# Order of the input stage's head, and the factor of the last norm, in a one-core decoder kernel

## Chip, core and metric

The kernel runs on one NeuronCore of one Trainium2 chip. The metric is the device time of one execution in microseconds (us), the median of several runs. Engines: PE (TensorE), DVE (VectorE), ACT (ScalarE), POOL (GpSimd), and SP, which here only issues transfers (DMAs).

## What is computed

One layer of a decoder runs over two groups of tokens that share the weights: a prompt of 1024 tokens and 8 single new tokens ("sample"). All is float32, the model width is 1024.

```python
def rmsnorm(x, g):
    return x * rsqrt(mean(x * x, -1) + 1e-6) * g

u = rmsnorm(h, norm_g) @ w_in                      # one wide projection, split into parts
o_r = rwkv_branch(first 1664 columns of u, ...)    # token-shift recurrence
o_n = nsa(...)                                     # sparse attention: compressed, selected, window
m = sigmoid(g_r) * ((o_r * silu(z_r)) @ proj_r) + sigmoid(g_n) * ((o_n * silu(z_n)) @ proj_n)
h = h + m @ w_out
h = h + sigmoid(h @ w_pg) * rmsnorm(p @ w_pe, pe_norm_g)
y = rmsnorm(h, final_norm_g)
```

The change touches the first line (the norm in front of the projection) and the last (the final norm of the prompt's last two tiles of 128 tokens).

## The kernel before

The kernel is a chain of stages (input projection, recurrence, token projection, attention, sample attention, merge, finish). Each stage is a block with a program per engine. The engines are ordered by semaphores only; a program waits with `wait_ge` and goes on in its own order. Between two stages stands one barrier, and semaphores of the stage before are cleared there (`Stage.clear`, L82). Each stage starts when the slowest engine of the one before is done.

**Input stage, `project_input`.** The tokens are nine tiles: eight of 128 prompt tokens, and one of 8. SP loads the tiles of `x`, five of the ten small vectors, and the first weights `w_z` (L751), in a queue written out by hand; ACT issues the other five vectors (L724). For each tile i:

- ACT squares the tile and sums (L938), and takes the root (L940, semaphore `rooted`).
- DVE takes the reciprocal (L1049) and scales the tile (L1051, `normed`).
- PE transposes it, eight blocks of 128x128 (`turn(i)`, L817, `turned`): four into one PSUM bank, four into the next.
- ACT copies the first four blocks to `xnT`, multiplying each by the norm's gain (L928, `out_a`); DVE copies the other four (L987, `out_v`).

The gain is a column of `vec`. The ten vectors land in `rows`, PE transposes them once (L893, `vec_t`), and DVE copies the result to `vec` (L981, `vec_o`). For the first three tiles the scaling of all three comes before the copies of all three; later tiles go one by one, and ACT and DVE copy tile i-1 behind their work on tile i.

PE then runs products of 344 tokens by 128 columns of weights over 8 blocks of the width (`product(u)`, L833); each block is two matmul instructions in the trace. The first product needs tiles 0 to 2. Turns of later tiles stand between and inside the products. Ahead of all that PE transposes the identity over and over (`keep_clock`, L122), 28 times before the vectors and 10 times behind them. Behind the plain products come pairs of products at L879.

**Finish stage, `finish_tokens`.** It goes over the tiles in four pairs. For the last pair (tiles 6 and 7; v = `NT - 2` and `NT - 1`), DVE makes the last sums of both: tile 6 in `gated_last` (L3910, L3912, `y0_l`), tile 7 in `gated` (L3901, L3903, `y0_v`), each in halves of 512 columns, the half of columns 512 to 1023 first. ACT squares each half and sums (L3776) and takes the root (L3786, `y_root`). DVE then runs `normed(v)`: the reciprocal (L3917) and two instructions of 512 columns that multiply by it and by the gain `gfin` (L3920, `y_out`). SP waits for `y_out` and stores tile by tile (L3554), the last tile in two halves (L3557). POOL has part of the sums of pairs 0 to 2 (L3851, L3853) and nothing in the last pair. `et` is a buffer of the gated rows, dead once the sums are made.

Of the kernel before, what the change touches and what calls it, by code (L numbers as in the profile page):

```python
# [15 lines left out]
ALU = mybir.AluOpType  # L16
# [3 lines left out]
P = 128  # L20
D = 1024
KC = D // P
# [24 lines left out]
NV = 51  # L47
# [621 lines left out]
def project_input(nc, k, x, o):  # L669
# [9 lines left out]
    with Stage(nc) as ctx:  # L679
# [61 lines left out]
        def turn_bank(i):  # L741
            return 6 if i == 0 or i > 2 else 6 - 2 * i
# [65 lines left out]
        def _(pe):  # L808
# [12 lines left out]
            def product(u):  # L821
# [5 lines left out]
                pe.wait_ge(out_v, last_tile + 1)  # L827
                if u >= 6:
                    pe.wait_ge(copied, u - 5)
                for c in range(KC):  # L830
                    if c == KC // 2 and u % 3 == 2 and u + 3 <= NT:
                        turn(u + 3)
                    last = nc.tensor.matmul(k.ps[:, u % 6, 0:CG], w[:, n % w_ring, c, :], k.xnT[:, c, g * CG:(g + 1) * CG],  # L833
                                            start=(c == 0), stop=(c == KC - 1))
# [56 lines left out]
            keep_clock(nc, k, 7, 28)  # L891
            pe.wait_ge(in_vec, 160)
            nc.tensor.transpose(k.ps[:, 0, 0:NV], rows[:], k.ident[0:NV, 0:NV]).then_inc(vec_t, 1)  # L893
            keep_clock(nc, k, 7, 10)
            for i in range(3):
                turn(i)
# [79 lines left out]
        def _(dve):  # L976
# [3 lines left out]
            dve.wait_ge(vec_t, 1)  # L980
            nc.vector.tensor_copy(k.vec[:], k.ps[:, 0, 0:NV]).then_inc(vec_o, 1)  # L981

            def turned_out(i):
                m = tokens(i)
                dve.wait_ge(turned, 2 * i + 2)
                for c in range(4):
                    last = nc.vector.tensor_scalar(k.xnT[:, 4 + c, i * P:i * P + m], k.ps[:, turn_bank(i) + 1, c * P:c * P + m],  # L987
                                                   k.vec[:, V_NG + 4 + c:V_NG + 5 + c], None, ALU.mult)
                last.then_inc(out_v, 1)
# [55 lines left out]
            dve.wait_ge(vec_o, 1)  # L1045
            for i in range(NT + 1):
                m = tokens(i)
                dve.wait_ge(rooted, i + 2)
# [2408 lines left out]
def finish_tokens(nc, k, x, o):  # L3457
# [8 lines left out]
    with Stage(nc) as ctx:  # L3466
# [30 lines left out]
        gm_l, y0_l = ctx.sem("gated_last"), ctx.sem("y_summed_last")  # L3497
        block = ctx.block()
# [29 lines left out]
        def _(sp):  # L3528
# [23 lines left out]
            for v in range(NT - 1):  # L3552
                sp.wait_ge(y_out, 2 * v + 2)
                sp.dma_start(o.y_prompt[0, tile_rows(v), :], h[:, v, :]).then_inc(k.y_stored[v % 2], 16)  # L3554
            for n in (1, 0):
                sp.wait_ge(y_out, 2 * NT - n)
# [278 lines left out]
        def _(pool):  # L3835
# [10 lines left out]
            for p in range(NPR - 1):  # L3846
                for n, half in enumerate((1, 0)):
# [5 lines left out]
                    nc.gpsimd.tensor_tensor(h[:, 2 * p, cols(half)], a, h[:, 2 * p, cols(half)], ALU.add).then_inc(y0_p, 1)  # L3853

        @block.vector
        def _(dve):
# [146 lines left out]
            normed(NT - 2)  # L4003
            normed(NT - 1)
# [150 lines left out]
```

## Time and profile before

| | us |
|---|---|
| median of 3 runs | 1676.46 |
| lowest and highest run | 1670.69, 1685.29 |
| the profiled execution | 1676.41 |
| its span, first to last instruction | 1674.6 |
| PE busy in the span | 1627.0 |

The mean granted TensorE clock of the span is 0.996. The busy time of an engine is the sum over its instructions; a wait is shown in front of the instruction that waited, with what released it. In a row such as `14.64 4.87 PE L833 ... x16` the first number is when the group starts, counted from the span's start, and the second how long it takes from first start to last end. "SPq" is the issue of a transfer, not its flight.

### The profile page before, as it was taken

The numbers are of one execution on the slowest core, as the hardware profiler recorded it, in microseconds if no ns is written. First come the engines' busy times: TensorE is split into PE (matmuls) and PEld (weight loads), VectorE is DVE, ScalarE is ACT, GpSimd is POOL, SyncE is SP. The second block draws the span as 40 slices with busy tenths as digits, with TensorE's granted clock in tenths as the row PEclk, the third lists the DMA queues.
The fourth block names the chain that finished last, engine by engine and source line by source line (L and its number), as shares of the span: only waits on it lengthen the run. The fifth ranks groups of instructions, "written<-read, shape, count | busy, mean of one in ns | idle before, by whom it ended". The sixth has DMA issues, their size and how long they took to land. (4 is left out here: it accounts for less than half of the span.)

```text
span 1674.6 us, 45562 instructions
## 1 busy us (share of the span) xinstructions
PE 1627.0 (97%) x20051; PEld 1163.7 (69%) x20051; DVE 854.1 (51%) x1790; ACT 577.1 (34%) x1244; POOL 396.1 (24%) x455
## 2 busy tenths in 40 slices
PE   8999999999999999999999999999999999999997
PEld 6788777777777555676767889765588888445443
DVE  3433555556565354767766664541152466624344
ACT  5221444454533114667663111223312211102444
POOL 0212223333331130556454220223100032000110
PEclk9999999999999999999999999999999999999999
DMA  5112000100101315712001975458611420700001
GB/s 169 39 50 57 3 17 16 29 17 17 29 17 36 93 29 138 218 51 101 2 2 71 293 293 197 155 139 198 157 25 27 140 62 1 277 1 1 25 26 50
DMA packets 111449, 136.80 MB, mean 82 GB/s; under 512 B 42940, under 2 KB 93829, under 8 KB 106046
## 3 DMA queue, kind: packets, MB, share of 16 engines
q1 hardware_dynamic: 102002, 84.61, 17.4%
q0 software_dynamic: 9216, 49.29, 9.5%
q8 instruction: 159, 2.61, 0.7%
q14 instruction: 36, 0.29, 0.1%
q10 hardware_dynamic: 36, 0.01, 0.0%
HBM read 121.28 MB, written 17.15 MB: 83 GB/s over the span
## 5 line engine op out<-in xcount | busy, mean ns | idle before, releaser
L1276 PE MATMUL ps<-xnT,rw_side_w 64*64 64x344 f32 x2304 | 219.3, 458 | 1.6 <-issue 0.9
L1276 PEld LDWEIGHTS ps<-xnT,rw_side_w 64*64 64x64 f32 x2304 | 97.2, 134 | 33.5 <-issue 12.4
L2744 PE MATMUL ps<-xnT,zT 128*128 128x344 f32 x384 | 120.1, 457 | 0.0
L2458 POOL TENSOR_SCALAR probs<-probs,row_sums,gates 128x63 f32<-128x63 f32 (+6 forms) x148 | 95.5, 666 | 94.9 <-DVE row_sums L2414 94.5
L2744 PEld LDWEIGHTS ps<-xnT,zT 128*128 128x128 f32 x384 | 69.5, 190 | 33.1 <-issue 3.4
L2363 ACT ACTIVATE probs<-probs,neg_max 128x63 f32<-128x63 f32 (+6 forms) x148 | 87.5, 595 | 0.3 <-DVE neg_max L2404 0.3
L2336 PE MATMUL ps<-probsT,kvtok 128*64 128x128 f32 x1056 | 76.2, 282 | 0.0
L2379 ACT ACTIVATE probsT<-ps 128x512 f32<-128x512 f32 (+1 forms) x80 | 45.9, 574 | 84.0 <-PE ps L2322 84.0
L2309 PE MATMUL ps<-kT,zT 64*128 64x512 f32 (+3 forms) x384 | 72.0, 484 | 2.2 <-DVE neg_max L2404 1.6
L3454 POOL TENSOR_TENSOR mT<-mT,gate_n 128x258 f32<-128x258 f32 x28 | 23.7, 854 | 210.9 <-DVE gate_n L3417 210.9
L2336 PEld LDWEIGHTS ps<-probsT,kvtok 128*64 128x64 f32 x1056 | 56.7, 138 | 24.2 <-issue 23.1
L2322 PE MATMUL ps<-ident,probs 128*128 128x128 f32 (+1 forms) x460 | 68.8, 281 | 4.8 <-DVE probsT L2435 3.2
L2435 DVE COPY probsT<-ps 128x512 f32<-128x512 f32 (+1 forms) x80 | 50.5, 631 | 37.3 <-PE ps L2322 36.4
L1804 POOL TENSOR_TENSOR rw_Lb<-rw_Lm,level_mask 128x512 f32<-128x512 f32 x40 | 54.0, 1359 | 49.9 <-PE ps L1458 33.0
L3353 ACT ACTIVATE zT<-ps 128x258 f32<-128x258 f32 x72 | 27.8, 387 | 106.5 <-PE ps L3335 83.7
L2322 PEld LDWEIGHTS ps<-ident,probs 128*128 128x128 f32 (+1 forms) x460 | 50.2, 141 | 17.7 <-issue 10.4
L3567 PE MATMUL ps<-w_sums,ring_k 128*128 128x512 f32 x128 | 57.2, 593 | 1.6 <-DVE h_tok L3880 1.6
L3335 PE MATMUL ps<-xnT,zT 128*128 128x258 f32 x256 | 57.6, 381 | 0.0
L1014 DVE TENSOR_TENSOR zT<-ps,zT 128x258 f32<-128x258 f32 x30 | 12.8, 426 | 82.3 <-PE ps L879 82.3
L879 PE MATMUL ps<-x_tok,z_sums 128*128 128x258 f32 x240 | 53.8, 381 | 0.0
L3335 PEld LDWEIGHTS ps<-xnT,zT 128*128 128x128 f32 x256 | 48.6, 190 | 7.1
L3880 DVE TENSOR_TENSOR h_tok<-ps,h_tok 128x512 f32<-128x512 f32 x28 | 19.3, 691 | 61.1 <-PE ps L3567 61.1
(625 smaller groups left out, 3584.6 us busy)
## 6 DMA issues: line engine op xcount, KB each, us to landing
w_z<-in_w_in_dram SPq DMA_DIRECT2D x13, 512.0 KB, 5.1
xnT_kept<-xnT SPq DMA_DIRECT2D x1, 4128.0 KB
x_tok<-in_x_prompt_dram SPq DMA_DIRECT2D x8, 512.0 KB, 7.0
rw_side_w<-in_w_in_dram SPq DMA_DIRECT2D x16, 256.0 KB, 3.4
zT<-in_w_in_dram SPq DMA_DIRECT2D x8, 512.0 KB, 6.1
ring_k<-in_w_in_dram SPq DMA_DIRECT2D x8, 512.0 KB, 5.2
w_out<-in_w_out_dram SPq DMA_DIRECT2D x1, 4096.0 KB
h_tok<-in_x_prompt_dram SPq DMA_DIRECT2D x8, 512.0 KB, 5.2
```

The source lines that it names most:

```text
L879: last = nc.tensor.matmul(k.ps[:, bank, 0:cq], left[:, c, :], right[:, c, :], start=(c == 0 and name in ("P1", "P5", "P2")), stop=(c == 3) ...
L1276: last = nc.tensor.matmul(k.ps[half(f), bank, 0:CG], w.side[half(e), g // 3 % 2, c, half(f)], k.xnT[half(e), c, third(g)], start=(phase == ...
L1804: nc.gpsimd.tensor_tensor(w.Lb[:, n % 2], w.Lm[:].rearrange("p q c n -> p (q c) n"), bc(k.tab["level_mask"][:, n + 1, :], 1, 8), ALU.mult) ...
L2309: last = nc.tensor.matmul(k.ps[:, 2 * (s % 2) + g, at:at + w], k.qT[half(g), j, i * P:(i + 1) * P], keys[half(g), t0:t0 + w], start=True, ...
L2322: last = nc.tensor.transpose(k.ps[0:m, 4 + pc % 2, (2 * b + g) * P:(2 * b + g + 1) * P], region(n, br, g, t * P, m), k.ident[:])
L2336: last = nc.tensor.matmul(k.ps[half(g), 6 + n % 2, 0:P], vals, pt[0:m, pc % NPT, (2 * b + g) * P:(2 * b + g + 1) * P], start=(br == 1 and ...
L2363: nc.scalar.activation(every, every, ACT.Exp, scale=-1.0, bias=neg_m[:, at:at + 1], accum_out=ls[:, at:at + 1]).then_inc(expd, 1)
L2435: nc.vector.tensor_copy(to, src).then_inc(pt_v, 1)
L2458: nc.gpsimd.tensor_scalar(every, every, ls[:, at:at + 1], k.gates[:, i, gate:gate + 1], ALU.mult, ALU.mult).then_inc(scaled, 1)
L2744: ins = self.nc.tensor.matmul(self.k.ps[:, self.banks[n % nb], 0:CG], self.w[:, t % 2, c, :], self.k.xnT[:, c, g * CG:(g + 1) * CG], start ...
L3335: last = nc.tensor.matmul(k.ps[:, bank, 0:CQ], stationary(u, n, name, c), moving(u, n, name, c, i), start=(c == 0 and name in ("P1", "P5", ...
L3567: last = nc.tensor.matmul(k.ps[:, bank, :], left[:, c, :], right[:, c, :], start=(first and c == 0), stop=(c == 3), skip_group_check=True)
```

## The change

In the input stage:

- PE makes 22 transposes of the identity instead of 28, then turns tile 0, then waits for the vectors and turns them, then tiles 1 and 2, then makes 8 more transposes of the identity (into bank 1) instead of the 10 that stood behind the vectors.
- DVE no longer copies the vectors before it norms the first tile, but between tiles 1 and 2.
- DVE's four copies of a tile by 128 columns become one multiply of 128x512 from PSUM, with the gain spread over the tokens.
- A product waits for ACT's half of the tiles at its start as before, but for DVE's half only in front of its fifth block.

In the finish stage, for tiles 6 and 7 only:

- They are multiplied by the gain before their roots are there: three halves on POOL (both of tile 6, the later columns of tile 7), one on DVE, all into `et`.
- DVE takes both reciprocals. POOL then scales all of tile 6 in one instruction (`y_pool`), DVE tile 7 in two halves.
- SP's store of tile 6 waits for POOL. The stores' order is the same: tile 6, then the two halves of tile 7.

The diff holds nothing about the barrier between stages; the kernel before has it already.

```diff
--- before
+++ after
@@ -824,10 +824,11 @@
                     pe.wait_ge(in_w[n % w_ring], 16)
                 last_tile = min(NT, ((g + 1) * CG - 1) // P)
                 pe.wait_ge(out_a, last_tile + 1)
-                pe.wait_ge(out_v, last_tile + 1)
                 if u >= 6:
                     pe.wait_ge(copied, u - 5)
                 for c in range(KC):
+                    if c == KC // 2:
+                        pe.wait_ge(out_v, last_tile + 1)
                     if c == KC // 2 and u % 3 == 2 and u + 3 <= NT:
                         turn(u + 3)
                     last = nc.tensor.matmul(k.ps[:, u % 6, 0:CG], w[:, n % w_ring, c, :], k.xnT[:, c, g * CG:(g + 1) * CG],
@@ -888,12 +889,13 @@
                 last.then_inc(last_t, 1)
 
             pe.wait_ge(eye_made, 1)
-            keep_clock(nc, k, 7, 28)
+            keep_clock(nc, k, 7, 22)
+            turn(0)
             pe.wait_ge(in_vec, 160)
             nc.tensor.transpose(k.ps[:, 0, 0:NV], rows[:], k.ident[0:NV, 0:NV]).then_inc(vec_t, 1)
-            keep_clock(nc, k, 7, 10)
-            for i in range(3):
-                turn(i)
+            turn(1)
+            turn(2)
+            keep_clock(nc, k, 1, 8)
             pe.wait_ge(vec_o, 1)
             for u in range(plain):
                 product(u)
@@ -977,16 +979,13 @@
             dve.wait_ge(zeroed, 5)
             nc.vector.memset(k.bdones[0:HD, 0:HD], 1.0).then_inc(made, 1)
             nc.vector.memset(k.bdones[HD:P, HD:P], 1.0).then_inc(made, 1)
-            dve.wait_ge(vec_t, 1)
-            nc.vector.tensor_copy(k.vec[:], k.ps[:, 0, 0:NV]).then_inc(vec_o, 1)
 
             def turned_out(i):
                 m = tokens(i)
                 dve.wait_ge(turned, 2 * i + 2)
-                for c in range(4):
-                    last = nc.vector.tensor_scalar(k.xnT[:, 4 + c, i * P:i * P + m], k.ps[:, turn_bank(i) + 1, c * P:c * P + m],
-                                                   k.vec[:, V_NG + 4 + c:V_NG + 5 + c], None, ALU.mult)
-                last.then_inc(out_v, 1)
+                src = k.ps[:, turn_bank(i) + 1, :].rearrange("p (c n) -> p c n", n=P)[:, :, 0:m]
+                nc.vector.tensor_tensor(k.xnT[:, 4:8, i * P:i * P + m], src, bc(k.vec[:, V_NG + 4:V_NG + 8], 2, m),
+                                        ALU.mult).then_inc(out_v, 1)
 
             def operand_sums(p, group):
 
@@ -1042,9 +1041,12 @@
                 nc.vector.scalar_tensor_tensor(out=z[:, mid - 1:TT], in0=s[:, mid - 1:TT], scalar=mu, in1=z[:, mid - 1:TT],
                                                op0=ALU.mult, op1=ALU.add).then_inc(mixed, 1)
 
-            dve.wait_ge(vec_o, 1)
             for i in range(NT + 1):
                 m = tokens(i)
+                if i == 2:
+                    dve.wait_ge(vec_t, 1)
+                    nc.vector.tensor_copy(k.vec[:], k.ps[:, 0, 0:NV]).then_inc(vec_o, 1)
+                    dve.wait_ge(vec_o, 1)
                 dve.wait_ge(rooted, i + 2)
                 nc.vector.reciprocal(sd[0:m, i:i + 1], sd[0:m, i:i + 1]).then_inc(rs_done, 1)
                 dve.wait_ge(rs_done, i + 1)
@@ -3495,6 +3497,7 @@
         gm_p, gm_v, y0_p, y0_v, y_sq, y_mid, y_root, y_rs, y_out = (ctx.sem(n) for n in (
             "gated_pool", "gated_dve", "y_summed_pool", "y_summed_dve", "y_squared", "y_half_mean", "y_rooted", "y_recip", "y_out"))
         gm_l, y0_l = ctx.sem("gated_last"), ctx.sem("y_summed_last")
+        yg_p, yg_v, y_pool = ctx.sem("y_gained_pool"), ctx.sem("y_gained_dve"), ctx.sem("y_out_pool")
         block = ctx.block()
 
         def cols(n):
@@ -3550,10 +3553,13 @@
             for t in range(4):
                 k.stores(sp.dma_start(o.y_sample[:, 0, t * Q:(t + 1) * Q], ys[32 * t + 24:32 * (t + 1), :]))
             for v in range(NT - 1):
-                sp.wait_ge(y_out, 2 * v + 2)
+                if v < NT - 2:
+                    sp.wait_ge(y_out, 2 * v + 2)
+                else:
+                    sp.wait_ge(y_pool, 1)
                 sp.dma_start(o.y_prompt[0, tile_rows(v), :], h[:, v, :]).then_inc(k.y_stored[v % 2], 16)
             for n in (1, 0):
-                sp.wait_ge(y_out, 2 * NT - n)
+                sp.wait_ge(y_out, 2 * NT - 2 - n)
                 sp.dma_start(o.y_prompt[0, tile_rows(NT - 1), cols(n)], h[:, NT - 1, cols(n)]).then_inc(k.y_stored[1], 16)
             k.stores.wait(sp)
             sp.wait_ge(k.y_stored[0], 16 * NPR)
@@ -3851,6 +3857,16 @@
                     nc.gpsimd.tensor_tensor(a, a, sg[:, p % 2, 0, cols(half)], ALU.mult).then_inc(gm_p, 1)
                     pool.wait_ge(gm_p, 2 * p + n + 1)
                     nc.gpsimd.tensor_tensor(h[:, 2 * p, cols(half)], a, h[:, 2 * p, cols(half)], ALU.add).then_inc(y0_p, 1)
+            p = NPR - 1
+            pool.wait_ge(y0_l, 1)
+            nc.gpsimd.tensor_tensor(et[:, p % 2, 0, cols(1)], h[:, NT - 2, cols(1)], gfin[:, cols(1)], ALU.mult).then_inc(yg_p, 1)
+            pool.wait_ge(y0_v, 2 * p + 1)
+            nc.gpsimd.tensor_tensor(et[:, p % 2, 1, cols(1)], h[:, NT - 1, cols(1)], gfin[:, cols(1)], ALU.mult).then_inc(yg_p, 1)
+            pool.wait_ge(y0_l, 2)
+            nc.gpsimd.tensor_tensor(et[:, p % 2, 0, cols(0)], h[:, NT - 2, cols(0)], gfin[:, cols(0)], ALU.mult).then_inc(yg_p, 1)
+            pool.wait_ge(yg_p, 3)
+            pool.wait_ge(y_rs, NT - 1)
+            nc.gpsimd.tensor_scalar(h[:, NT - 2, :], et[:, p % 2, 0, :], ms[:, 2, NT - 2:NT - 1], None, ALU.mult).then_inc(y_pool, 1)
 
         @block.vector
         def _(dve):
@@ -4000,8 +4016,18 @@
                 if p == NPR - 1:
                     gated_last(0, 1)
             gated(NPR - 1, 0, 1)
-            normed(NT - 2)
-            normed(NT - 1)
+            p = NPR - 1
+            dve.wait_ge(y0_v, 2 * NPR)
+            nc.vector.tensor_tensor(et[:, p % 2, 1, cols(0)], h[:, NT - 1, cols(0)], gfin[:, cols(0)], ALU.mult).then_inc(yg_v, 1)
+            for v in (NT - 2, NT - 1):
+                r = ms[:, 2, v:v + 1]
+                dve.wait_ge(y_root, v + 1)
+                nc.vector.reciprocal(r, r).then_inc(y_rs, 1)
+            dve.wait_ge(y_rs, NT)
+            dve.wait_ge(yg_v, 1)
+            dve.wait_ge(yg_p, 2)
+            for n in (1, 0):
+                nc.vector.tensor_scalar(h[:, NT - 1, cols(n)], et[:, p % 2, 1, cols(n)], ms[:, 2, NT - 1:NT], None, ALU.mult).then_inc(y_out, 1)
 
 
 def hybrid_trunk(nc, tables, ins, outs):
```

## Rows read from the trace of the kernel before

**Rows 1.** The page, part 1: busy us, share of the span, instructions of each engine
```profile
PE 1627.0 (97%) x20051; PEld 1163.7 (69%) x20051; DVE 854.1 (51%) x1790; ACT 577.1 (34%) x1244; POOL 396.1 (24%) x455
```

**Rows 2.** Busy time by stretches, PE: stretch, length, busy (instructions), PEclk, DMA share, GB/s
```profile
19.70:61.00 41.30, 41.30 (x174) 1.00 0.18 43
```

**Rows 3.** Order of time, the head: start us, us, engine, line, operation, [idle before]
```profile
1.99 5.98 PE L122 MATMUL ps<-ident 128*128 128x128 f32 x28 [1.99 <-POOL ident L788]
...
5.75 0.29 ACT L940 ACTIVATE x_sd<-x_ss,x_eps 128x1 f32<-128x1 f32 x1
...
8.18 0.26 PE L893 MATMUL ps<-ident,vec_rows 51*128 51x51 f32 x1 [0.21 <-DMA vec_rows<-in_rwkv_k_k_dram]
...
8.48 0.21 DVE L981 COPY vec<-ps 128x51 f32<-128x51 f32 x1 [6.72 <-PE ps L893]
...
8.48 0.29 ACT L940 ACTIVATE x_sd<-x_ss,x_eps 128x1 f32<-128x1 f32 x1
...
8.92 0.75 DVE L1051 TENSOR_SCALAR x_tok<-x_tok,x_sd 128x1024 f32<-128x1024 f32 x1
...
10.48 3.21 ACT L928 ACTIVATE xnT<-ps,vec 128x128 f32<-128x128 f32 x12 [1.71 <-PE ps L817]
...
11.31 3.19 DVE L987 TENSOR_SCALAR xnT<-ps,vec 128x128 f32<-128x128 f32 x12
...
14.64 4.87 PE L833 MATMUL ps<-xnT,w_z 128*128 128x344 f32 x16 [2.07 <-DVE xnT L987]
```

**Rows 4.** Line L122, 7.4 to 7.6 us: duration ns min/median/max
```profile
L122 PE MATMUL ps<-ident x3: 273/377/421, 7.2 to 7.6; 128*128 128x128 f32 x3
```

**Rows 5.** Line L751, the transfers issued at 4.05 and at 5.61, each alone
```profile
DMA to landing us min/median/max: 5.1/5.1/5.1
...
DMA to landing us min/median/max: 7.8/7.8/7.8
```

**Rows 6.** Order of time, the tail
```profile
1664.00 0.69 DVE L3912 TENSOR_TENSOR h_tok<-w_out,h_tok 128x512 f32<-128x512 f32 x1
...
1666.69 0.69 DVE L3903 TENSOR_TENSOR h_tok<-w_out,h_tok 128x512 f32<-128x512 f32 x1
...
1668.18 0.29 ACT L3786 ACTIVATE mean_sq<-mean_sq 128x1 f32<-128x1 f32 x1
...
1669.10 0.16 DVE L3917 RECIPROCAL mean_sq<-mean_sq 128x1 f32<-128x1 f32 x1
...
1669.21 0.33 SPq L3554 DMA_DIRECT2D out_y_prompt_dram<-h_tok  x1
...
1669.29 1.41 DVE L3920 SCALAR_TENSOR_TENSOR h_tok<-h_tok,mean_sq,g_final 128x512 f32<-128x512 f32 x2
...
1670.07 0.99 SPq L3557 DMA_DIRECT2D out_y_prompt_dram<-h_tok  x2
```

**Rows 7.** The last stores: DMA by stretches (as rows 2), and issue to landing
```profile
1670.00:1671.00 1.00, 0.00 (x0) 0.50 0.98 389
...
out_y_prompt_dram<-h_tok SPq DMA_DIRECT2D x2, 256.0 KB, 2.5
```

**Rows 8.** Groups by form, POOL and DVE: line, operation | busy us, mean ns
```profile
L3851 POOL TENSOR_TENSOR w_out<-w_out 128x512 f32<-128x512 f32 x6 | 7.6, 1265 | 130.5 <-ACT w_out L3768 130.5
...
L2458 POOL TENSOR_SCALAR probs<-probs,row_sums,gates 128x1024 f32<-128x1024 f32 x8 | 9.5, 1204 | 22.0 <-DVE row_sums L2414 22.0
...
L1860 DVE TENSOR_SCALAR rw_kp<-rw_aa,vec,omka 128x512 f32<-128x512 f32 x8 | 4.2, 528 | 0.0
...
L1997 DVE TENSOR_TENSOR rw_Gbr<-ps,gmask 128x512 f32<-128x512 f32 x8 | 5.4, 679 | 0.0
```

**Rows 9.** Order of time at 590.9 us: DVE beside POOL
```profile
590.91 1.70 POOL L373 TENSOR_TENSOR cmp_w1b<-xnT 128x512 f32<-128x512 f32 x1 [14.03 <-PE ps L438]
...
590.92 0.56 DVE L578 TENSOR_TENSOR dist_near<-w_kv,cmp_w1b 128x396 f32<-128x396 f32 x1
...
591.40 1.64 DVE L578 TENSOR_TENSOR p_small<-w_kv,cmp_w1b 128x396 f32<-128x396 f32 x1
```

## The prediction

> **What bounds the kernel now.** I read the page first. TensorE (PE) is busy for 97% of the span [rows 1], and there is one core, so an edit counts only where PE waits, or after PE's last matmul. The diff touches two such places: the first 15 us, and the tail behind the last sums of the last two tiles.
>
> Second, the busy time by stretches and the order of time in the head. In front of the first product (L833) PE waits 2.07 us for VectorE's (DVE's) copies at L987 [rows 3]. From there it has no hole: between 19.7 and 61 us it is busy for all 41.3 us [rows 2]. So what the first product gains is kept to the end of the stage, and each later stage starts at a barrier and moves along.
>
> Third, what makes those copies late [rows 3]. DVE stands at L981 until PE has turned the vector rows at 8.18, for which PE waits on a DMA. Only then does it norm tile 0, though the root of tile 0 was ready at 5.75 + 0.29 = 6.04. Tile by tile that delay is handed down: ScalarE's (ACT's) twelve copies begin at 10.48 and end at 13.69, DVE's twelve begin at 11.31 and end at 14.50, and the product starts 0.14 later, at 14.64.
>
> Fourth, the tail [rows 6]. The last sum of the last tile ends at 1667.38, its root at 1668.47. But DVE first finishes tile 6, so tile 7's reciprocal starts at 1669.10 and its two halves end at 1670.70. SP issues the store of tile 6 at 1669.21 and the two halves from 1670.07; the second goes out at about 1670.73.
>
> **The head, step by step.**
> - PE's opening transposes: 28 take 5.98 us, 0.214 each, so 22 end at 1.99 + 4.70 = 6.7. The six removed and the ten removed behind the vectors were cover, not work; eight come back behind turn(2).
> - Tile 0 normed without the vectors: 6.04, reciprocal 0.16, scaling 0.75, with the handovers 7.02. PE waits from 6.7 to 7.1.
> - turn(0), eight transposes. Their pace is the open cost. A transpose takes 421 ns, start to end, up to about 7.4 us and 273 ns after it [rows 4]: PE goes from the lower level (1.2 GHz) to the upper (2.4 GHz) at 7.4 to 7.6, having been busy since 1.99. In pace that is 0.214 against 0.11 a transpose. turn(0) ends at 7.1 + 8 x 0.11 = 8.0 at best and at 7.1 + 8 x 0.214 = 8.8 at worst. I take 8.2, a rise near 7.5 as now. The vectors (by DMA not before 8.18) then turn at 8.2, where they do now.
> - DVE has normed tile 1 before the vectors are turned, copies the vectors by 8.7 [rows 3], and norms tile 2: root ready at 8.77, so 8.80 + 0.16 + 0.75 and a handover = 9.75, against 11.4 now. What queues behind DVE's new wait for the vectors is this tile 2 and the copies, and both need it anyway.
> - ACT is free when the root of tile 2 is done, at 8.77; vec_o is up at 8.7 and turn(0) is done. Its twelve copies take 3.21 and end at 12.0 instead of 13.69. turn(2) runs 9.8 to 10.7, in time for the last four.
> - DVE's copies are now three of 128x512 from PSUM. The nearest form, a 128x512 multiply from PSUM, takes 0.68 [rows 8], so three take about 1.9 from 9.8 and end near 11.7. The upper bound is the old 3.19: 13.0. Even that is hidden, because the product asks for DVE's half only at its fifth block, 2.4 us in. If that cover were gone it would cost 0.9.
> - The eight transposes behind turn(2) end at 11.6, before the product may start.
> - The product starts when ACT is done, plus 0.14: 12.15 against 14.64, **2.5 us earlier**. With turn(0) slow to the end, the vectors turn at 8.8, ACT runs 9.4 to 12.6, and the gain is 1.9.
> - Transfers: the first weights are issued at 4.05 and land 5.1 later, at 9.2; the second are issued at 5.61 and land 7.8 later, at 13.4, and are wanted at about 17.7 [rows 5]. SP's queue is unchanged in the head.
>
> **The tail, step by step.** Two things change: tiles 6 and 7 are multiplied by the gain while the roots are taken, and tile 6 is finished on GpSimd (POOL).
> - POOL's three multiplies at 1.27 each [rows 8]: the last waits for tile 6's second sum, which ends at 1664.69 [rows 6], so it ends at 1666.0, hidden under the last tile's own sums; the other two start behind earlier sums.
> - DVE after 1667.38: the gain of half a tile 0.69 (to 1668.1), reciprocal of tile 6 (to 1668.2), reciprocal of tile 7 after its root at 1668.47 (to 1668.67).
> - POOL scales tile 6, 1024 columns. No such instruction stands in this stage; the nearest POOL form is a 128x1024 scaling in another stage, 1204 ns [rows 8]. The upper bound is two POOL 512-wide multiplies, 2.53. I take 1.2, the same operation and size. It starts near 1668.35 and ends at **1669.55**, where now the store of tile 6 is issued at 1669.21. It is late by 0.35.
> - DVE scales tile 7's halves. A 128x512 scaling takes 0.53 [rows 8]. Free to run from 1668.7 they would end at 1669.7, a full 1.0 before now.
> - But both stores of tile 7 stand behind tile 6's on SP (0.33 each). The last then goes out at 1669.58 + 0.33 + 0.35 = 1670.3 instead of 1670.73: 0.4 earlier.
> - And the three stores move 1.05 MB at 389 GB/s, 2.7 us [rows 7], in one unbroken run that begins with tile 6's. That run starts 0.35 later. So the tail lies between -0.4 (the last store's flight of 2.5 us decides) and +0.35 (bandwidth decides). I take **0**: what tile 7 gains, tile 6 pays.
>
> A further row speaks against the free DVE. While POOL had a multiply under way (590.91, 1.70 instead of 1.27), DVE's two-input multiply that started at 591.40 took 1.64 where its neighbour took 0.56, and ended only after POOL's [rows 9]. If DVE's scaling waits for POOL in this way, the halves end at about 1670.1 and 1670.6, and the last store goes out 0.1 earlier than now, not 0.4.
>
> The Trainium skill, "SBUF — State Buffer", section "Who interferes with whom", says that GpSimd and certain Vector instructions, tensor_scalar in its two-port modes and those with two SBUF inputs among them, lock one shared port pair for a whole instruction. For two inputs the trace agrees (1.64 against 0.56); for the scaling no row of this trace shows it. By that rule the tail gives 0.1, without it 0.4.
>
> **Sum.** The profiled execution took 1676.41 us (span 1674.6), the median of the runs is 1676.46, so the two can be used as one. 1676.4 - 2.5 + 0 = **1673.9**. The title's single barrier isn't in the diff, so it is costed at nothing.
>
> **The rivals.**
> - *The tail is faster than I say.* Tile 7's early factor shows in full, 1.0 us, because tile 6's store doesn't hold it up. For it: DVE's own work is 1.0 shorter. Against: SP's order and the 2.7 us of data. Time 1672.9. Chance 0.10.
> - *Tile 6 on POOL is the new bound.* At 2.53 instead of 1.2 its store goes out 1.7 late and the data run ends 1.7 later: 1676.4 - 2.5 + 1.7 = 1675.6. For it: POOL takes 1.27 for 512 columns with two inputs. Against: one input and 1.2 in the row. Chance 0.12.
> - *The head gains only part.* PE's hole from 6.7 to 7.1 comes just before the rise that the old order got at 7.5. If PE stays at the lower level a little longer, turn(0), turn(1) and turn(2) run at 0.214, to 12.5, and the eight filler transposes at L122 queue in front of the product to 14.2. Gain 0.4 to 1.9; time about 1675.2. Chance 0.13.
> - *Slower than before*, by the same mechanism carried further: the clock is still low when the product starts at 14.2. Each us at half pace loses 0.5 us, so beyond 15.1 the gain is gone; with the whole first product low it takes 9.2 instead of 4.7, ends 4.1 later than now: 1680.5. For it: transposes are short and PE now has three small holes in the head. Against: now it stands idle from 12.6 to 14.6 and starts the product at full pace. Chance 0.05.
> - *Nothing is gained*, because a later wait swallows the head's 2.5. Against it: no hole of PE from 19.7 to 61. Time 1676.4. Chance 0.05.
>
> **How the numbers follow.** My forecast, 1673.9 with its own range 1673.2 to 1674.9 in one execution, has 0.55. All cases but one lie between 1672.9 and 1676.4. But the three runs before lie from 1670.69 to 1685.29, a spread of 14.6 us, many times the effect; a median of three can fall some 5 us off either way. That, not the bounds, sets the range: 1667 to 1682. A measurement of this kernel can tell about 1%, 16.8 us, from no change. No case reaches that: faster by over 1% 0.03, slower 0.03 (both only by the spread of the runs), within 1% 0.94.
>
> **What the changed profile would show.** Head: L833 begins near 12.1 (steps right) or 14.2 (clock late); ACT's L928 copies begin at 8.8; transposes of turn(0) change from 421 to 273 ns within it; three DVE multiplies of about 0.68 replace twelve; PE stays whole behind the first product. Tail: the POOL scaling of tile 6 takes 1.2 and ends near 1669.5 less 2.5; DVE's first scaling of tile 7 either ends 0.5 after 1668.7 less 2.5 or waits for POOL; the last store is issued 0.1 to 0.4 nearer to the last matmul's end than now, and the data of the three stores is one run. A POOL scaling of 2 us or more, a first product past 13 us, or a hole of PE in front of a product from 17 to 60 us would make the prediction wrong.

## The result, and the profile after

The changed kernel is slower by about 6 us, and not faster by 2.5.

| | before | after |
|---|---|---|
| median of 20 runs each, us | 1676.04 | 1681.87 |
| lowest to highest | 1670.57 to 1685.29 | 1676.91 to 1694.72 |
| ratio, 95% interval | | 1.0032 (1.0016 to 1.0047) |
| profiled execution, us | 1676.41 | 1678.74 |
| its span, mean granted clock | 1674.6, 0.996 | 1676.7, 0.993 |

The ratio is taken within rounds and says +5.4 us; the medians differ by 5.8. Both lie within 1% of no change. The time lies at the upper edge of the range, on the other side of "no change" from the forecast.

On the page, the engines' busy time tells almost nothing of it (columns as in [rows 1]):

```profile
PE 1624.2 (97%) x20043; PEld 1163.2 (69%) x20043; DVE 849.4 (51%) x1762; ACT 576.3 (34%) x1244; POOL 402.1 (24%) x459
```

PE has eight matmuls fewer, and is busy 2.8 us less, in a span that is 2.1 longer. So in this execution the loss is idle time of PE. (It is among the faster of its kernel's, 2.3 us above before's, where the medians are 5.8 apart.) Three places matter.

**The head** came out as forecast. Order of time, the head of after (columns and places as [rows 3]):

```profile
7.11 1.09 PE L817 MATMUL ps<-ident,x_tok 128*128 128x128 f32 x8 [0.51 <-DVE x_tok L1053]
...
8.26 0.26 PE L895 MATMUL ps<-ident,vec_rows 51*128 51x51 f32 x1
...
9.09 3.18 ACT L930 ACTIVATE xnT<-ps,vec 128x128 f32<-128x128 f32 x12
...
10.16 1.96 DVE L987 TENSOR_TENSOR xnT<-ps,vec 128x512 f32<-128x512 f32 x3
...
12.42 4.87 PE L834 MATMUL ps<-xnT,w_z 128*128 128x344 f32 x16 [0.15 <-ACT xnT L930]
```

The first product starts at 12.42 instead of 14.64, 2.2 us earlier.

**The tail** did not. Order of time, the end of after (as [rows 6]), and below it the two scalings of tile 7 by line (duration ns min/median/max, then the first and the last start):

```profile
1668.26 2.86 POOL L3869 TENSOR_SCALAR h_tok<-w_out,mean_sq 128x1024 f32<-128x1024 f32 x1 [2.33 <-DVE mean_sq L4025]
...
1668.61 1.43 DVE L4030 TENSOR_SCALAR h_tok<-w_out,mean_sq 128x512 f32<-128x512 f32 x2
...
1671.15 0.33 SPq L3560 DMA_DIRECT2D out_y_prompt_dram<-h_tok  x1
...
1671.52 1.27 SPq L3563 DMA_DIRECT2D out_y_prompt_dram<-h_tok  x2
```

```profile
L4030 DVE TENSOR_SCALAR h_tok<-w_out,mean_sq x2: 476/756/1035, 1668.6 to 1669.6; 128x512 f32<-128x512 f32 x2
```

POOL needs 2.86 us for tile 6, not 1.2. DVE's two scalings of tile 7 end at 1669.6 and 1670.0, but all three stores wait behind POOL, until 1671.15. From the end of PE's last matmul to the end of the span it is 11.54 us, against 9.34 before: 2.2 us later.

**A hole in the middle**, which the prediction did not have. The diff touches nothing there. It lies in sample attention, in the values of the window, a loop of 160 short matmuls. Order of time of PE, after:

```profile
1117.64 1.99 PE L2987 MATMUL ps<-ring_v,s_win 128*32 128x64 f32 x128
1119.57 0.54 PE L2993 MATMUL ps<-row_s,n_win 8*32 8x64 f32 x24
1122.97 0.44 PE L2993 MATMUL ps<-row_s,n_win 8*32 8x64 f32 x8 [2.87 <-issue]
```

and of before, the same two loops:

```profile
1123.79 1.99 PE L2985 MATMUL ps<-ring_v,s_win 128*32 128x64 f32 x128
1125.71 0.65 PE L2991 MATMUL ps<-row_s,n_win 8*32 8x64 f32 x32
```

After stops inside one line, for 2.87 us, with 24 of 32 matmuls done. The releaser is "issue": it waited for no semaphore. Behind the hole the granted clock is at half for 6.8 us. Busy time by stretches of after (columns as [rows 2]):

```profile
1119.60:1122.20 2.60, 0.50 (x28) 1.00 0.51 124
1122.30:1129.10 6.80, 6.12 (x25) 0.50 0.63 116
1129.20:1133.00 3.80, 3.55 (x28) 1.00 0.60 138
```

while before runs through it at the upper level (1123 to 1126: busy 3.00 of 3.00, clock 1.00). The hole costs 2.9 us, and half pace over 6.8 us another 3.4: together some 6.3. Lined up by what the engines do, after is 6 us ahead of before when the burst starts, and 0.1 ahead at 1130. Of the 6 us the head gave 2.2, and some 1.7 is low clock that before had more of by then (10.2 us of it against 6.8). The rest arose for the most part between 210 and 355 us, in the recurrence, and is not separated here.

What came in during the hole is seen in the queues. DMA queues (packets, MB, busy share), after, first 1117.7 to 1120.1 and then 1120.1 to 1123.0:

```profile
q0 software_dynamic: 155, 0.54, 103.6%
```

```profile
q0 software_dynamic: 62, 0.19, 23.6%
q8 instruction: 1, 0.02, 2.9%
```

The one packet of the "q8 instruction" queue starts at 1120.24, 0.1 us after PE stopped. In before the packet of this place starts at 1122.97, 0.8 us ahead of the 160 matmuls (1123.79). Over a whole execution of either kernel that queue shows:

```profile
q8 instruction: 159, 2.61, 0.7%
```

That is 16 KB a packet. The trace of before has 40,797 instructions of PE, that of after 40,777 (20,051 and 20,043 matmuls, as many weight loads, the rest waits and the like); 40,797 / 159 = 256.6. I read this as PE's program, fetched in pieces of 256 instructions. (At this point that is an inference from the count; the section "How the place acts" tests it.) In after PE goes on 2.7 us after the packet's start (1120.24 to 1122.97), while the whole burst, 320 instructions and so more than one piece, takes 2.5 us. So a packet that starts late in the burst leaves PE standing. And the change moves the border between pieces within the burst: eight transposes fewer (16 instructions) and four instructions of waits fewer put everything behind the head 20 instructions earlier.

### The profile page after: what moved, and what is told of

Read it like the earlier page. It is cut to its first block and busy times, and to the rows that moved or that the text cites. A ratio compares the mean times of both kernels' runs of the same rounds, so it can differ in the third digit from the quotient of the medians.

```text
span 1676.7 us, 45522 instructions
## 1 busy us (share of the span) xinstructions
PE 1624.2 (97%) x20043; PEld 1163.2 (69%) x20043; DVE 849.4 (51%) x1762; ACT 576.3 (34%) x1244; POOL 402.1 (24%) x459
## 5 line engine op out<-in xcount | busy, mean ns | idle before, releaser
L1278 PE MATMUL ps<-xnT,rw_side_w 64*64 64x344 f32 x2304 | 215.5, 455 | 1.2 <-issue 0.6
```

What stands on the lines that cost most here:

```text
L1278: last = nc.tensor.matmul(k.ps[half(f), bank, 0:CG], w.side[half(e), g // 3 % 2, c, half(f)], k.xnT[half(e), c, third(g)], start=(phase == ...
```

## The experiments

The theory: three terms, a head of -2.2, a tail of +2.2, and a hole of some +6 that hangs on the place of the burst in PE's program and on nothing else of the change. The rivals: the hole is chance, or comes of the new order or timing of the head; the tail is slow since POOL and DVE lock each other out, or by the change of buffer. Runs that stand together in a table below shared their runs of before; the median of before moved between 1672.75 and 1677.88 from group to group, so only differences within a group count. In the tables "us" is the difference of the medians. The ratio is taken within rounds and can say something else: for a1 it is 1.0032, which is 5.4 us, where the medians are 1.8 apart.

### Undo the place, and make it alone

*a1_padded*: the changed kernel, with PE's program made as long again as before by 40 waits that are already met, which compile to 20 instructions, ahead of the filler transposes at the end of the head:

```diff
+            for _ in range(40):
+                pe.wait_ge(eye_made, 1)
             keep_clock(nc, k, 2, 26)
```

> The changed kernel with 40 waits that are already satisfied put in front of PE's last filler transposes of the input stage. They become 20 instructions, so that all of PE's later program stands at the same place in memory as in the kernel before (the change had moved it 20 instructions forward). Theory A (where PE's program is cut into the 16 KB pieces that are loaded): PE's 2.9 us issue gap at L2993 and the 6.8 us at half clock behind it are gone, and the time falls by about 6 us, to about 1676, level with before (head -2.2, tail +2.2). Rival B (the head's new order or a chance in the clock costs it): the time stays near 1682.

*a2_before_short*: the kernel before, with only ten of those transposes taken out, 20 instructions:

```diff
-            keep_clock(nc, k, 2, 26)
+            keep_clock(nc, k, 2, 16)
```

> The kernel before with 16 instead of 26 filler transposes at the end of the input stage: 20 PE instructions fewer, nothing else. Theory A: an issue gap of some 3 us appears at L2991 with a stretch at half clock behind it, and the time is about 6 us above before, near 1682. Rival B: no change, 1676; rival C (the filler at that place matters for the clock): the low stretch is at 190 us, not at 1120.

*a3_tail_only* and *a4_head_only*: the kernel before with one half of the diff each. a3 has the hunks from line 3497 on (tile 6 on POOL, both gains early), among them

```diff
+            nc.gpsimd.tensor_scalar(h[:, NT - 2, :], et[:, p % 2, 0, :], ms[:, 2, NT - 2:NT - 1], None, ALU.mult).then_inc(y_pool, 1)
```

and a4 those up to line 1053 (the head), among them

```diff
-            keep_clock(nc, k, 7, 28)
+            keep_clock(nc, k, 7, 22)
+            turn(0)
```

> The kernel before with only the finish stage of the change. PE's program is unchanged. POOL's scaling of tile 6 takes 2.9 us as in the changed kernel and the span's end lies 2.2 us further behind the last matmul: 1678.2. If the scaling takes 1.2 us, as the prediction took it, the time is that of before.

> The kernel before with only the input stage of the change; PE's later program is 20 instructions further forward. Theory A: head -2.2, gap and low clock at L2993 +6, so about 1680. Theory B': the head alone gains 2.2, no gap at L2993: 1674.

| | median | before | ratio (95%) | us | hole at the burst |
|---|---|---|---|---|---|
| a1 | 1675.75 | 1673.96 | 1.0032 (1.0008 to 1.0057) | +1.8 | 0.37 |
| a2 | 1680.24 | 1673.96 | 1.0040 (1.0012 to 1.0067) | +6.3 | 3.08 |
| a3 | 1676.19 | 1673.96 | 1.0024 (1.0004 to 1.0043) | +2.2 | 1.36 |
| a4 | 1675.13 | 1673.96 | 1.0013 (0.9994 to 1.0032) | +1.2 | 3.25 |

a2 is the decisive one. It holds nothing of the change, only the shift, and has the same hole after the same 24 matmuls, with the same half clock behind it. Order of time of PE in a2, and a stretch of it:

```profile
1124.79 0.54 PE L2991 MATMUL ps<-row_s,n_win 8*32 8x64 f32 x24
1128.40 0.44 PE L2991 MATMUL ps<-row_s,n_win 8*32 8x64 f32 x8 [3.08 <-issue]
```

```profile
1128.40:1134.00 5.60, 5.60 (x23) 0.50 0.65 111
```

It is 6.3 us slower than before, though it does less. Fewer fill transposes could also have cost clock where they stand, and in a2's profile the low stretches at 192 and at 964 us do last 6.8 us each, instead of 3.4. But a2 still stands 0.9 us ahead of before when the burst starts, and 5.0 behind at 1134, so that in this execution the loss is made at the burst. a1 is the whole change at the old place, and the hole shrinks to 0.37:

```profile
1121.98 0.49 PE L2995 MATMUL ps<-row_s,n_win 8*32 8x64 f32 x18 [0.37 <-issue]
```

That kills both rivals for the hole: a1 has the new head and no large hole, a2 the old head and the large one. a1's time, though, should have been level with before and was 1.8 above it, by its ratio as far above as the changed kernel is; 5 of its 12 runs were over 1682. Its profiled execution took 1674.97. So a1's verdict rests on its trace alone: in the time, it does not show that the loss is undone. The granted clock that stands with every run says what the slow ones lack. a1's five runs over 1682 had a mean clock of 0.984 to 0.990, its other seven 0.994 to 0.996, and 0.006 of 1675 us is 10 us. Why its clock was low more often is open, since those five left no trace.

The same figure for the other kernels: the median granted clock was 0.996 for before in each of the three large groups, 0.993 to 0.994 for after, a2 and e1 (the changed kernel again, below), 0.995 for a4, and 0.996 or more for b4, b1 and e3, which have the shift undone as a1 has (a1: 0.994). 0.003 of 1675 us is 5 us (an estimate; some of the low clock falls behind the last matmul, where it costs nothing). So in the runs as in the traces low clock is a large part of the loss.

a3 is the tail alone, +2.2 (by the ratio +4.0, interval 0.7 to 7.2); its end shows 2.2 (11.54 us behind the last matmul, against 9.34). a4 has the large hole and the old end (9.35), and lost less than expected: its low clock behind the hole lasted 3.4 us, not 6.8.

### The head without the two losses, and another tail

*b4_head_padded*: a4 with a1's padding.

> Input stage of the change, finish stage of before, and the 20 PE instructions put back, so that the later program stands where it stood. Theory A: the head's 2.2 to 2.6 us are kept to the end, no issue gap in the sample attention: 2.4 us below before (0.15%). Theory D (the new order costs more low clock later on, as the padded kernel's median of 1.8 above before suggests): not below before.

*b3_dve_tile6*: the kernel before with the new tail, but DVE scales tile 6 itself.

```diff
-            nc.gpsimd.tensor_scalar(h[:, NT - 2, :], et[:, p % 2, 0, :], ms[:, 2, NT - 2:NT - 1], None, ALU.mult).then_inc(y_pool, 1)
...
+                if v == NT - 2:
+                    dve.wait_ge(y_rs, NT - 1)
+                    dve.wait_ge(yg_p, 3)
+                    nc.vector.tensor_scalar(h[:, v, :], et[:, p % 2, 0, :], ms[:, 2, v:v + 1], None, ALU.mult).then_inc(y_pool, 1)
```

> The kernel before with that finish stage alone. Span's end 8.7 to 9.0 us behind the last matmul instead of 9.34; time 0.3 to 0.6 below before, which the runs cannot tell from none. If tile 6's POOL scaling was not the cause of the 2.2 us, it stays at 11.5.

*b1_best*: b4 and b3 together.

> As the run before it, and the finish stage of the change with one edit: DVE instead of POOL scales tile 6 (1024 columns, 0.75 us by its form in the input stage). Tile 6's store then goes out at about 3.6 us behind the last matmul, where before has 3.9, and the last half at 4.8 instead of 5.4. The end of the span lies 0.3 to 0.6 us nearer to the last matmul than before (9.34): 8.7 to 9.0. Total: 2.9 us below before (0.17%); under theory D not below before.

| | median | before | ratio (95%) | us |
|---|---|---|---|---|
| b4 | 1675.46 | 1677.88 | 0.9974 (0.9951 to 0.9998) | -2.4 |
| b3 | 1677.23 | 1677.88 | 1.0003 (0.9989 to 1.0016) | -0.7 |
| b1 | 1676.81 | 1677.88 | 0.9991 (0.9968 to 1.0014) | -1.1 |

b4 shows the head's gain alone, in the time: -2.4 us (by the ratio -4.4, interval -8.2 to -0.3). It is the only kernel here that is faster than before by more than its interval. b3 has the order the change wanted, tile 6 first and tile 7 close behind (order of time, its end):

```profile
1665.54 0.75 DVE L4024 TENSOR_SCALAR h_tok<-w_out,mean_sq 128x1024 f32<-128x1024 f32 x1
...
1666.32 0.33 SPq L3558 DMA_DIRECT2D out_y_prompt_dram<-h_tok  x1
...
1666.40 0.88 DVE L4029 TENSOR_SCALAR h_tok<-w_out,mean_sq 128x512 f32<-128x512 f32 x2
...
1666.91 1.05 SPq L3561 DMA_DIRECT2D out_y_prompt_dram<-h_tok  x2
```

Yet its end is 9.29 us behind the last matmul, 0.05 better than before, where 8.7 to 9.0 was expected. DVE is done early, and nothing comes of it: the three stores and their data set the end. It comes 5.57 us after tile 6's store goes out in every kernel with the new tail (after, a3, b2, b3, d1, d2), and 5.41 in before. And tile 6's store goes out barely earlier in b3 (3.7 us behind the last matmul instead of 3.9). There was next to nothing to win in this tail. b1 should have been b4 with a little more; its interval covers both that and nothing. Its profiled execution had 27 us at half clock near 1073, far from anything changed, so it shows nothing more of the head or tail.

### Why POOL took 2.86

Three kernels, each the old head with the new tail (a3) and one thing changed. *b2_pool_alone*: DVE waits until POOL is done.

```diff
+            dve.wait_ge(y_pool, 1)
             for n in (1, 0):
```

> The kernel before with the finish stage of the change, but DVE waits for POOL's scaling of tile 6 before it scales tile 7. POOL then has its port to itself. Theory L (the 2.86 us are 1.2 of work and the rest a lock against DVE's two scalings): it takes 1.2. Theory S (POOL is simply slow in this form): it stays near 2.8. Either way DVE's halves take 0.5 each.

*d1_pool_two_factors*: the same product, with a second factor of ones.

```diff
-            nc.gpsimd.tensor_scalar(h[:, NT - 2, :], et[:, p % 2, 0, :], ms[:, 2, NT - 2:NT - 1], None, ALU.mult).then_inc(y_pool, 1)
+            nc.gpsimd.tensor_scalar(h[:, NT - 2, :], et[:, p % 2, 0, :], ms[:, 2, NT - 2:NT - 1], k.ones[:, 0:1], ALU.mult, ALU.mult).then_inc(y_pool, 1)
```

> The kernel before with the finish stage of the change, POOL's scaling of tile 6 by two factors from memory (the root's reciprocal and a column of ones) instead of one: the form of the row at L2458 from which 1.2 us was taken, except that it writes another buffer than it reads. If the form makes the price, it takes 1.2; if the buffers do, 2.8.

*d2_pool_in_place*: POOL writes to the buffer that it reads, and SP stores from there.

```diff
-                sp.dma_start(o.y_prompt[0, tile_rows(v), :], h[:, v, :]).then_inc(k.y_stored[v % 2], 16)
+                src = et[:, 1, 0, :] if v == NT - 2 else h[:, v, :]
+                sp.dma_start(o.y_prompt[0, tile_rows(v), :], src).then_inc(k.y_stored[v % 2], 16)
...
-            nc.gpsimd.tensor_scalar(h[:, NT - 2, :], et[:, p % 2, 0, :], ms[:, 2, NT - 2:NT - 1], None, ALU.mult).then_inc(y_pool, 1)
+            nc.gpsimd.tensor_scalar(et[:, p % 2, 0, :], et[:, p % 2, 0, :], ms[:, 2, NT - 2:NT - 1], None, ALU.mult).then_inc(y_pool, 1)
```

> The same with one factor as in the change, but in place (the store then reads that buffer). If writing elsewhere makes the price it takes 1.2; if the number of factors does, 2.8. If both this and the other stay at 2.8, the price is DVE's or the stage's.

Order of time, the end of each: b2, then d1, then d2.

```profile
1669.09 2.86 POOL L3867 TENSOR_SCALAR h_tok<-w_out,mean_sq 128x1024 f32<-128x1024 f32 x1 [2.33 <-DVE mean_sq L4023]
1672.08 0.88 DVE L4029 TENSOR_SCALAR h_tok<-w_out,mean_sq 128x512 f32<-128x512 f32 x2 [2.69 <-POOL h_tok L3867]
```

```profile
1666.96 1.19 POOL L3867 TENSOR_SCALAR h_tok<-w_out,mean_sq,ones 128x1024 f32<-128x1024 f32 x1 [2.33 <-DVE mean_sq L4023]
...
1667.31 1.52 DVE L4028 TENSOR_SCALAR h_tok<-w_out,mean_sq 128x512 f32<-128x512 f32 x2
```

```profile
1662.85 2.86 POOL L3868 TENSOR_SCALAR w_out<-w_out,mean_sq 128x1024 f32<-128x1024 f32 x1 [2.32 <-DVE mean_sq L4024]
```

Alone, beside DVE, in place or not, it is 2.86; with a second factor, that computes the same values, it is 1.19. The price is that of the form of the instruction. No lock and no buffer is behind it. The end of d1's span comes 9.87 us behind the last matmul, so of the tail's 2.2 us 1.7 are this one instruction. The other 0.5 stays: POOL's chain is still later than DVE's was.

### How the place acts

*c1_before_10*: before with five transposes fewer, 10 instructions.

```diff
-            keep_clock(nc, k, 2, 26)
+            keep_clock(nc, k, 2, 21)
```

> The kernel before with 21 instead of 26 filler transposes at the end of the input stage: 10 PE instructions fewer. Theory A: the piece's edge lies halfway; the gap at L2991 is between the two groups or in the longer one, 1.7 to 3.3. A single look.

*c3_before_p236*: before with 472 met waits, 236 instructions more, which is 20 fewer by a count modulo 256.

```diff
+            for _ in range(472):
+                pe.wait_ge(eye_made, 1)
             keep_clock(nc, k, 2, 26)
```

> The kernel before with 472 satisfied waits (236 instructions) at the end of PE's input stage. 236 forward the other way round is the same place in a piece of 256 as 20 instructions fewer. Theory A: although PE's program is longer instead of shorter, the gap at L2991 is that of the shifted kernels, 2.9 to 3.3 us, not that of the unshifted (0 to 1.7). The waits themselves may cost some us; only the gap is read. If the gap is 0 to 1.7, the cut into pieces of 256 is not the cause.

c3's hole, order of time of PE:

```profile
1155.20 0.31 PE L2993 MATMUL ps<-row_s,n_win 8*32 8x64 f32 x8 [3.62 <-issue]
```

Longer by 236 instructions instead of shorter by 20, and PE stops after the same 24 matmuls of the same line, for 3.62 us. This is what pieces of 256 instructions ask for, and no account by the amount of work gives it. It also has one packet more than all others on that queue, which shows that the queue carries PE's program:

```profile
q8 instruction: 160, 2.62, 0.6%
```

Its time of 1707.27 (before: 1675.57) says nothing of the hole: the 472 waits themselves left a gap of 22.7 us at the fill they stand in front of. c1 had no hole where 1.7 to 3.3 was expected: the border does not act in proportion. (Its one time, 1680.11, lies high by low-clock stretches elsewhere.)

*e1_after_same* is the changed kernel once more, with no edit. *e2_after_plus10* has half of a1's padding, 10 instructions:

```diff
+            for _ in range(20):
+                pe.wait_ge(eye_made, 1)
```

and *e3_after_pad_two_factors* is a1 with d1's edit.

> The changed kernel itself, beside the next two on one chip. Theory A: gap of about 3 us at L2993, low clock behind it, about 6 us above before.

> The changed kernel with PE's later program moved by 10 instructions only (20 satisfied waits at the end of the input stage). In the kernel before, 10 instructions fewer left no gap; so theory A expects none or a short one here and a time 5 to 6 us below the changed kernel's, level with before (head -2.4, tail +2.2). If what counts is to stand exactly as before, or if the cause is elsewhere, the time is the changed kernel's.

> The changed kernel with all 20 instructions put back and POOL's scaling of tile 6 by two factors (1.2 us instead of 2.9). Head -2.4; the end 9.9 behind the last matmul instead of 9.34 (+0.5): about 1.9 below before, and 7 to 8 below the changed kernel. This is the kernel that the prediction described.

| | median | before | ratio (95%) | us | hole | behind last matmul |
|---|---|---|---|---|---|---|
| e1 | 1677.12 | 1672.75 | 1.0021 (1.0002 to 1.0040) | +4.4 | 3.20 | |
| e2 | 1673.46 | 1672.75 | 1.0007 (0.9982 to 1.0031) | +0.7 | 0.82 | |
| e3 | 1670.25 | 1672.75 | 0.9987 (0.9968 to 1.0007) | -2.5 | 1.09 | 9.87 |

e1 has the loss again, hole and low clock included, so it is no chance of one execution. Ten instructions back (e2) take most of it away (3.7 us between the medians of e1 and e2, which ran in one group; the intervals of their ratios overlap); e3, with both causes mended, has the lowest median of its group (-2.5, -1.9 expected), although its interval still touches no change.

Where PE stops follows the place exactly. In after 24 of the 32 matmuls of that line are done, in a1 14, and in e2, half way back, 19 (order of time of PE in e2):

```profile
1119.29 0.52 PE L2995 MATMUL ps<-row_s,n_win 8*32 8x64 f32 x19
1120.62 0.42 PE L2995 MATMUL ps<-row_s,n_win 8*32 8x64 f32 x13 [0.82 <-issue]
```

Each matmul has a weight load, so 10 instructions are five matmuls. Counted from the start of the trace, PE stops behind its instruction 35,777 in 13 of the 14 profiles with a hole, whatever else they changed, and behind 36,033 in c3, which is 256 more. That is the border between two pieces. And in all 14 PE goes on 2.5 to 2.8 us after the start of the one packet that falls near the burst. So the hole is what is left of those 2.7 us at the moment when PE reaches the border:

| place | kernels | done of 32 | packet starts, us | hole, us | half clock behind it, us |
|---|---|---|---|---|---|
| same | before, d2 | no stop | 3.2, 2.7 ahead | 0, 0 | none |
| same | a1, b1, b2 | 14 | 2.3, 2.2, 1.8 ahead | 0.37, 0.65, 0.89 | none |
| same | e3, a3 | 14 | 1.7, 1.3 ahead | 1.09, 1.36 | none |
| same | d1, b4, b3 | 14 | 1.4, 1.0, 1.1 ahead | 1.39, 1.73, 1.74 | 3.4 each |
| -10 | c1 | no stop | 3.1 ahead | 0 | none |
| -10 | e2 | 19 | 1.8 ahead | 0.82 | none |
| -20 | after, a2, e1 | 24 | 0.14, 0.45, 0.44 behind | 2.87, 3.08, 3.20 | 6.8 each |
| -20 | a4 | 24 | 0.7 behind | 3.25 | 3.4 |
| +236 | c3 | 24 | 1.0 behind | 3.62 | 3.4 |

("Ahead" is before PE comes to the border, "behind" after it has stopped there.) All five at the shifted place have 2.87 to 3.62, all twelve others 0 to 1.74. What decides when the packet starts I did not test. Just ahead of the hole in after the transfers of the sample attention's gathers fill the DMA engines (the 103.6% above), and whether the packet waits for them is a rival that no run here separates from the place. It also means that a kernel at the old place isn't free of the burst: b4's profiled execution lost 1.7 there and some 1.7 more to the clock behind it.

The burst is not the only place. Each profile has 21 to 31 pauses of PE of over 0.1 us put down to "issue", 8.6 to 14.5 us in sum (10.6 in before, 12.5 in after; c3 apart), and others also follow the shift, both ways. Near 446 us all five shifted kernels pause for 0.6 to 0.8 us, and of the ten at the old place one does, for 0.5. Near 355 us none of the five does, and the ten do for 0.2 to 0.9. So what a shift is worth is a sum over all such places. This burst is the largest that moved.

## Why the prediction was wrong

- **Head, right.** First product at 12.42 instead of 12.15, since ACT's copies began at 9.09 and not 8.8: turn(0) was done at 8.2 as said, but ACT had to wait 0.27 for tile 2's load before it summed that tile, and its root ended at 9.18. In the other kernels with this head the product starts at 11.94 to 12.83. DVE's three multiplies took 1.96 (1.9 said). The clock rose inside turn(0) (its first transpose took 327 ns, the others 273), so the rival of a late clock is out. Gain 2.2 of 2.5, and b4 shows it in the time, -2.4.
- **"What the first product gains is kept, and each later stage moves along", wrong.** This step looked at waits: semaphores, barriers, transfers. It took PE's work behind the head to be untouched because its code is untouched. But its place in the program had moved by 20 instructions, and at one burst that costs a hole of 2.9 us and 3.4 us of half pace. "No hole of PE from 19.7 to 61" [rows 2] was true of before and of after, and could not tell of 1120. The rival "a later wait swallows the gain" had the effect and a chance of 0.05, with a price of 2.5 at most, where it was some 6.
- **POOL's scaling at 1.2, wrong by 1.7.** It took 2.86. The row for it stands in [rows 8], as `probs<-probs,row_sums,gates`: two factors. The one in the change has one. I called it "the same operation and size" and the number of operands in the row said otherwise. The rival with 2.53 had the mechanism right, with a price 0.3 too low (2.53 was put down as the upper bound, from two-input multiplies, and was none): it had the store of tile 6 go out 1.7 late, and it went out 1.9 late (1671.15 against 1669.21, with the last matmul ending within 0.1 us of before's). The prediction named a POOL scaling of 2 us or more as a thing that would make it wrong, and it did.
- **DVE's freedom, in part right.** The forecast had tile 7's halves done 1.0 earlier when undisturbed. They were done 0.7 earlier, at 1670.0 against 1670.7, because the first took 1.04 and not 0.53; the stores behind SP's wait for POOL made nothing of it. That tile 7 pays for tile 6 was right, and b3 shows that the gain of this tail was near zero from the start.
- **The lock between POOL and DVE.** In d1 DVE's first scaling took 1.13 instead of its neighbour's 0.47 and ended 0.3 us behind POOL's. This is the pattern of [rows 9]. In after the first took 1.04 and the second 0.48, and they ended 1.5 and 1.1 us ahead of POOL's. The Trainium skill, "SBUF — State Buffer", section "Who interferes with whom", has the lock last for a whole instruction; d1 agrees with that, and after does not: with POOL's slow form DVE was held for half a microsecond and then let through.
- **The sum.** Forecast -2.5 + 0 = -2.5. Measured by parts: -2.4 (b4) + 2.2 (a3) + 6.3 (a2) = +6.1; measured whole, +5.8 and, in another group, +4.4 (e1). The parts add up, but each is known to some us only, and two combinations fit less well: head and shift (a4) gave +1.2 where +3.9 follows, and head and tail at the old place (a1) +1.8 where 0 follows.
- **The range.** Its reason, the spread of the runs, was right. But it held no case of a loss of 6, and a slower outcome had been put down to the clock of the head alone. That rival's time, 1680.5, lies near the measured one by luck: nothing of its mechanism was seen.

What stays open: what decides when the packet starts, and with it why it comes 2.6 to 3.5 us after the burst's start at the shifted place, and from 0.8 before to 1.4 after it at all others; why holes of about the same length are followed by 0, 3.4 or 6.8 us of half clock; and why a1's clock was low in 5 of 12 runs.

## What to carry to other kernels

Where an engine runs a long unrolled program, an edit changes two things: what it says, and the place of all that stands behind it. Look in the trace for the densest bursts of short instructions behind the edit, and compare them before and after; a hole named "issue" inside one line, with a packet of the instruction queue in it, is the sign, and a few met waits ahead of the stage are enough to test it. When a price is taken from a nearby row, compare the number of operands and not only operation and shape.

## What the runs showed of the hardware

- PE's program came in 16 KB packets, 159 of them, and 160 when it was 236 instructions longer (c3). A burst of 160 short matmuls with their weight loads (320 instructions in 2.5 us) met a hole at the border between two pieces of 256 instructions: PE stopped behind its instruction 35,777 in 13 profiles and behind 36,033 in c3.
- PE went on 2.5 to 2.8 us after the start of the packet (14 profiles). The hole was 2.9 to 3.6 us at the shifted place and 0 to 1.7 elsewhere.
- Behind the eight longest holes (1.39 us and more) the granted clock fell from 1.00 to 0.50 for 3.4 or 6.8 us, with PE busy; behind the six shorter ones, up to 1.36 us, it did not. A hole of 2.9 us cost about 6 in after.
- Forty waits that are already met left no gap in front of the fill behind them (a1, b4); 472 of them left PE idle for 22.7 us (c3).
- POOL's scaling of 128x1024 in f32 took 2.86 us with one factor per partition (after, b2, d2) and 1.19 with two (d1, e3).
- Beside POOL's two-factor scaling DVE's 128x512 scaling took 1.13 us and ended behind POOL's (d1); beside the one-factor form it took 1.04 and ended 1.5 us ahead of it (after). Its neighbours took 0.47 and 0.48.
